# Grouped mixture-of-experts on sorted tokens: five slots of 128 tokens in place of sixteen experts on all 256, and the split of the down weights moved to GpSimd

## The chip, the cores and the metric

One core of a Trainium2 chip runs the whole program in one launch. The metric is device time in microseconds (us), less is better. TensorE does the matmuls, VectorE and ScalarE the elementwise work, GpSimd little, SyncE issues most DMAs. In the profile they are PE (PEld for its weight loads), DVE, ACT, POOL and SP; a "q" behind an engine's name is its instruction queue.

## The reference, cut to what matters

Two layers (projections, retention, windowed and latent attention, layer norm, mixture of experts, layer norm) and one block of another kind (attention, a linear recurrence, an MLP) run over 256 tokens of width 1024, in fp32. The change touches the experts of the two layers:

```python
def grouped_moe(x, router_w, router_bias, w_gate_up, w_down):   # 256 tokens, D = 1024
    scores = sigmoid(t @ router_w)                  # 16 experts in 4 groups of 4
    biased = scores + router_bias
    grp_score = sum(top_k(biased by group, 2))
    sel_group = argmax(grp_score)                   # one group for each token
    top_idx = top_k(biased inside that group, 2)    # two experts of that group
    gates = one_hot(top_idx) * scores / their sum
    h = einsum('td,edf->tef', t, w_gate_up)         # every expert: 1024 -> 2 x 256
    a = silu(h[..., :256]) * h[..., 256:] * gates
    y = einsum('tef,efd->td', a, w_down)            # 256 -> 1024, summed over experts
```

All of a token's weight lies on two experts of one group; for the other fourteen its gate is zero.

## The kernel before, in words

A Fori loop over the two layers holds all engines' programs; the last block follows it. Big matmuls take each fp32 operand as a rounded fp32r part ("high") and the rest ("low") and add three products: high by high, high by low, low by high. So every weight block of 128x2048 is loaded from HBM (by SP, into a half of WE), rounded by ScalarE (`high_up` L654, `high_down` L658), and its rest is taken by VectorE as a `tensor_tensor` subtract with both inputs in SBUF (`low_up` L1539, `low_down` L1543).

For each of the 16 experts all 256 tokens are computed. `expert_up` makes gate and up with the weights stationary and the tokens moving (96 matmuls of 256 columns); ScalarE takes silu (L798); VectorE multiplies with the gate values (L1669) and with the up part (L1673) and splits the result (L1534, L1535). `expert_down` adds 24 matmuls of 512 columns into four banks, y0 to y3, that stay open over all experts. `split_product` and `split_down` call `product`, whose matmul is L990. TensorE's program interleaves experts (`expert_up(m, 0)`, `expert_down(m - 1, 1)`, ...), and three pairs of high and low buffers (gate, up, down) make the other engines wait for TensorE and for one another. Gate values go by DRAM: transposed by TensorE (L1301), written out and broadcast back by two DMAs of the ACT queue (L785, L789).

SP loads an expert's gate and up (2 MB) in one DMA and its down (1 MB) in another, each as soon as the rest of the expert two before is taken (L456, L460). Before the experts come layer norm 1, `transpose_rows("x1T", ...)`, the router product (L990 on `small`), and the selection on VectorE (L1638 to L1664). `keep_warm(job, l, n)` issues n fp32 matmuls of 128 columns on an identity (L1031); an fp32 matmul is two instructions in the trace. After the experts `layer_norm` adds y0 to y3 (L1469 to L1483), and the next layer starts with loads into WE, `high_unit` (L691), `low_unit` (L1558 on VectorE, L547 on GpSimd) and `transpose_rows("xT", ...)`.

GpSimd's program: two `low_unit`, small loads, four `low_unit`, rotary products (L569 to L589), for each layer; then a memset of `w_bd` (L594) and 18 small DMAs (L599, L612) for the last block, on whose `final_in` ScalarE and VectorE wait before its first row is normed; then `low` of the last block's projections (L619).

Of the kernel before, what the change touches and what calls it, by code (L numbers as in the profile page):

```python
# [8 lines left out]
P = 128  # L9
SEQ, D, NL = 256, 1024, 2  # L10
T = SEQ // P
KD = D // P
# [5 lines left out]
PER_GRP = N_EXP // N_GRP  # L18
ST_H, CONV, D_FF, LRU_W = 8, 4, 4096, 512
# [40 lines left out]
    ("router", 0), ("gatesT", 1),  # L60
    ("y0", 0), ("y1", 1), ("y2", 2), ("y3", 3),
    ("gate0", 4), ("up0", 5), ("gate1", 6), ("up1", 7),
# [26 lines left out]
REPEATED = {"gate0": N_EXP // 2, "up0": N_EXP // 2, "gate1": N_EXP // 2, "up1": N_EXP // 2,  # L89
            "ff0": N_CHUNK // 2, "ff1": N_CHUNK // 2}  # L90

# [11 lines left out]
def tables():  # L103
# [26 lines left out]
    for e in range(PER_GRP):  # L130
# [9 lines left out]
        "before": (i < j).astype(np.float64),  # L140
        "tie": np.broadcast_to(tie.reshape(1, -1), (P, PER_GRP * PER_GRP)),
# [22 lines left out]
def build(nc, a, out):  # L164
    ctx = ExitStack()
    with ctx:
# [25 lines left out]
        small = sb("small", [P, 1400])  # L192
# [19 lines left out]
        QL = [over("QL0", "WA", UNIT, [P, KD, 256]), over("QL1", "XT", 0, [P, KD, 256]), over("QL2", "AC", AC_LATE + UNIT, [P, KD, 256])]  # L212
        HIDH = [over(f"HIDH{s}", "XT", s * 1024, [P, 2, SEQ]) for s in range(2)]
# [28 lines left out]
        for s in range(2):  # L242
            ar = Arena(WE, s * E_SLOT)
            w_gu.append(ar.take(KD, 2 * D_EXP))
            w_dn.append(ar.take(D_EXP // P, D))
        w_gate, w_up = ([w[:, :, n * D_EXP:(n + 1) * D_EXP] for w in w_gu] for n in range(2))
# [11 lines left out]
        ar = Arena(WB)  # L258
        gates_b = ar.take(N_EXP, SEQ)
        sig = [ar.take(512) for _ in range(2)]  # L260
        gatesT = ar.take(SEQ)
        assert ar.at <= 3 * UNIT
# [41 lines left out]
        gsel, esel, gden, gates = ar.take(8), ar.take(8, 4), ar.take(2), ar.take(2, N_EXP)  # L304
        n1g, n2g = ar.take(KD), ar.take(KD)
# [4 lines left out]
        rss, marks = ar.take(T), ar.take(8 + T + 2 + T)  # L310
# [4 lines left out]
        gates_dram = nc.dram_tensor("gates_scratch", [NL, N_EXP, SEQ], F32, kind="Internal").ap()  # L315
# [40 lines left out]
        norms_in, ln1_in, ln2_in, gates_in, gates_out = (sem(n) for n in ("norms_in", "ln1_in", "ln2_in", "gates_in", "gates_out"))  # L356
        gu_in, dn_in = [sem(f"gu_in{s}") for s in range(2)], [sem(f"dn_in{s}") for s in range(2)]
# [13 lines left out]
        gates_ready, expert_used = sem("gates_ready"), sem("expert_used")  # L371
# [4 lines left out]
        xt_high, xt_low = sem("xt_high"), sem("xt_low")  # L376
# [21 lines left out]
        DVE_LINKS, POOL_LINKS, MOE_LINKS = 32, 2, 2  # L398

        SLOT_UNITS = (N_EXP + 1, N_EXP, N_EXP - 1, 0)  # L400

        def unit(slot, l, e):
            return l * SLOT_UNITS[slot] + e + 1 if SLOT_UNITS[slot] else e + 1
# [7 lines left out]
        def hidden(l, e):  # L411
            return l * N_EXP + e + 2
# [5 lines left out]
        def _(sp):  # L418
            for t in range(T):
                sp.dma_start(X[:, t, :], a["x"][0, t * P:(t + 1) * P, :]).then_inc(x_in[t], 16)  # L420
            with sp.Fori(0, NL) as l:
# [3 lines left out]
                sp.wait_ge(hid_ready, l * N_EXP + 1)  # L425
# [3 lines left out]
                sp.wait_ge(psum_read[3], l * per_layer[3] + 1)  # L429
# [25 lines left out]
                def load_gate_up(e, s):  # L455
                    sp.dma_start(w_gu[s], a["exp_w_gate_up"][bass.ds(l, 1), bass.ds(e, 1)].rearrange(  # L456
                        "o e (p k) n -> p (o e k) n", k=KD)).then_inc(gu_in[s], 16)

                def load_down(e, s):
                    sp.dma_start(w_dn[s], a["exp_w_down"][bass.ds(l, 1), bass.ds(e, 1)].rearrange(  # L460
                        "o e (c p) n -> p (o e c) n", p=P)).then_inc(dn_in[s], 16)

                for s in range(2):
                    load_gate_up(s, s)
                    load_down(s, s)
# [3 lines left out]
                with sp.Fori(1, N_EXP // 2) as m:  # L469
                    for s in range(2):  # L470

                        sp.wait_ge(low_made[1], unit(1, l, 2 * m + (s - 2)))
                        load_gate_up(2 * m + s, s)

                        sp.wait_ge(low_made[2], unit(2, l, 2 * m + (s - 2)))
                        load_down(2 * m + s, s)
            w2 = a["w_in_2"][0].rearrange("(p k) n -> p k n", k=KD)
            for p, col in enumerate(PROJ_PAIRS):
                if p < 2:

                    sp.wait_ge(low_made[1], unit(1, NL - 1, N_EXP - 2 + p))
# [52 lines left out]
        def _(pool):  # L534
# [5 lines left out]
            with pool.Fori(0, NL) as l:  # L540
# [51 lines left out]

            pool.wait_ge(k_roped, NL + 1)
# [45 lines left out]
        def _(act):  # L639
# [20 lines left out]
            def split_xt(prefix, l):  # L660
                for n in range(4):
# [1213 lines left out]
```

## Time and profile before

| | us |
|---|---|
| median of 3 runs (lowest, highest) | 1242.46 (1239.92, 1244.7) |
| profiled execution, its own time | 1242.1 |
| its span in the trace | 1240.4 |
| PE busy in the span | 1187.7 (96%) |
| DVE, ACT, POOL busy | 641.2, 464.5, 157.2 |
| mean granted clock of TensorE, share of full | 0.986 |
| DMA traffic | 193.94 MB |

Read: the first two lines are times of the whole program; the span is what the trace shows of it. Busy TensorE is not TensorE at its peak, since a matmul's row is longer than the step from one matmul to the next.

### The profile page before, as it was taken

How to read it: one execution, taken by the hardware profiler on the slowest of the kernel's cores; microseconds unless marked ns; L12 is line 12 of the kernel's file. 1: busy time of each engine (PE TensorE's matmuls, PEld its weight loads, DVE VectorE, ACT ScalarE, POOL GpSimd, SP SyncE). 2: the span in 40 equal slices, each digit the busy share in tenths (PEclk: the TensorE clock that was granted, in tenths of full speed). 3: DMA queues.
4: the chain of work that ended last, by engine and by line, in shares of the span. 5: the costliest groups of instructions: out<-in, count | busy, mean ns of one | idle time of the engine just before them, and what ended most of it. 6: DMA issues, size and time to landing. Idle time of an engine off the chain costs nothing.

```text
span 1240.4 us, 19509 instructions
## 1 busy us (share of the span) xinstructions
PE 1187.7 (96%) x7992; PEld 1057.1 (85%) x7992; DVE 641.2 (52%) x721; ACT 464.5 (37%) x533; POOL 157.2 (13%) x90
## 2 busy tenths in 40 slices
PE   8997999999999999996999999999999989999998
PEld 8985579999999989965498999999989865899997
DVE  2226566565555554056566655555564843655653
ACT  3423323333333333432333333333343864443431
POOL 2433000000000003616000000000046420000000
PEclk9997999999999999997999999999999999999999
DMA  9702634554444338107254554445414035355431
GB/s 314 195 2 87 252 103 171 203 203 193 162 161 194 135 105 237 67 1 235 113 192 183 203 198 164 158 190 203 169 35 170 1 136 203 136 203 195 170 141 68
DMA packets 78562, 193.94 MB, mean 156 GB/s; under 512 B 17648, under 2 KB 48544, under 8 KB 74032
## 3 DMA queue, kind: packets, MB, share of 16 engines
q1 hardware_dynamic: 76368, 184.23, 40.8%
q10 hardware_dynamic: 640, 6.27, 1.3%
q0 software_dynamic: 1504, 2.73, 0.9%
q8 instruction: 36, 0.59, 0.2%
q14 instruction: 14, 0.11, 0.0%
HBM read 192.14 MB, written 1.08 MB: 156 GB/s over the span
## 4 chain that ended last, share of the span: by engine, by line
PE 80%; DVE 7%; issue 6%; ACT 3%; DMA 2%; POOL 1%; DVEq 0%; POOLq 0%; ACTq 0%
PE bank L990 73%; PE bank L1031 2%; DMA WB<-gates_scratch 1%; DVE LNB L1791 1%; PE bank L1083 1%; DVE WA L1517 1%; DMA gates_scratch<-WB 1%; DVE AC L1749 1%; PE bank L1065 1%; POOL QL L547 1%; PE bank L1044 0%; ACT WH L654 0%; PE bank L1190 0%; PE bank L1059 0%; PE bank L1069 0%
## 5 line engine op out<-in xcount | busy, mean ns | idle before, releaser
L990 PE MATMUL bank<-XTH,WH 128*128 128x256 f32 x1280 | 362.8, 283 | 1.3 <-DVE XTL L1734 0.8
L990 PE MATMUL bank<-XTH,WL 128*128 128x256 f32 x1280 | 362.2, 283 | 0.0
L990 PE MATMUL bank<-XTL,WH 128*128 128x256 f32 x1280 | 362.2, 283 | 0.0
L990 PEld LDWEIGHTS bank<-XTH,WH 128*128 128x128 f32 x1280 | 245.5, 192 | 3.5 <-issue 1.0
L990 PEld LDWEIGHTS bank<-XTL,WH 128*128 128x128 f32 x1280 | 245.5, 192 | 1.6
L990 PEld LDWEIGHTS bank<-XTH,WL 128*128 128x128 f32 x1280 | 245.5, 192 | 0.0
L1539 DVE TENSOR_TENSOR WL<-WE,WH 128x2048 fp32r<-128x2048 f32 x80 | 183.1, 2291 | 38.3 <-ACT WH L654 36.3
L654 ACT CAST WH<-WE 128x2048 fp32r<-128x2048 f32 x80 | 151.9, 1903 | 105.7 <-PE bank L990 95.3
L1543 DVE TENSOR_TENSOR WL<-WE,WH 128x2048 fp32r<-128x2048 f32 x48 | 109.9, 2290 | 85.4 <-ACT WH L658 85.4
L990 PE MATMUL bank<-WH,HIDH 128*128 128x512 f32 x384 | 150.3, 391 | 3.1 <-DVE HIDL L1535 1.8
L658 ACT CAST WH<-WE 128x2048 fp32r<-128x2048 f32 x48 | 91.5, 1906 | 158.1 <-PE bank L990 149.2
L990 PE MATMUL bank<-WL,HIDH 128*128 128x512 f32 x384 | 149.9, 390 | 0.0
L990 PE MATMUL bank<-WH,HIDL 128*128 128x512 f32 x384 | 149.4, 389 | 0.0
L547 POOL TENSOR_TENSOR QL<-WE,QH 128x2048 fp32r<-128x2048 f32 (+2 forms) x12 | 48.5, 4060 | 414.4 <-ACT QH L691 414.4
L619 POOL TENSOR_TENSOR PL<-WE,PH 128x2048 fp32r<-128x2048 f32 x10 | 46.7, 4676 | 364.5 <-ACT PH L833 364.5
L990 PEld LDWEIGHTS bank<-WH,HIDH 128*128 128x128 f32 x384 | 72.3, 188 | 17.6 <-issue 2.2
L990 PEld LDWEIGHTS bank<-WH,HIDL 128*128 128x128 f32 x384 | 72.1, 188 | 15.3
L990 PEld LDWEIGHTS bank<-WL,HIDH 128*128 128x128 f32 x384 | 72.3, 188 | 13.3
L1031 PE MATMUL bank<-tab 128*128 128x128 f32 x536 | 67.5, 286 | 7.2 <-DMA tab<-in_tables 5.4
L1031 PEld LDWEIGHTS bank<-tab 128*128 128x128 f32 x536 | 66.0, 203 | 9.2 <-issue 9.1
L990 PE MATMUL bank<-WB,XT 128*128 128x512 f32 x160 | 70.0, 595 | 3.6 <-ACT XT L757 1.7
L990 PE MATMUL bank<-XTH,QH 128*128 128x256 f32 x224 | 64.0, 286 | 1.3 <-POOL QL L547 0.8
(288 smaller groups left out, 1626.6 us busy)
## 6 DMA issues: line engine op xcount, KB each, us to landing
WE<-in_exp_w_gate_up SPq DMA_DIRECT2D x32, 2048.0 KB, 9.0
WE<-in_exp_w_down SPq DMA_DIRECT2D x32, 1024.0 KB, 4.9
WE<-in_w_up SPq DMA_DIRECT2D x16, 1024.0 KB, 5.2
WE<-in_w_down SPq DMA_DIRECT2D x16, 1024.0 KB, 5.6
WE<-in_w_in SPq DMA_DIRECT2D x7, 2048.0 KB, 9.4
WE<-in_w_in SPq DMA_DIRECT2D x8, 1024.0 KB, 8.7
WB<-in_w_out SPq DMA_DIRECT2D x2, 2560.0 KB, 10.5
WB<-gates_scratch ACTq DMA_DIRECT2D x2, 2048.0 KB, 8.6
```

What stands on the lines that cost most here:

```text
L547: nc.gpsimd.tensor_tensor(QL[u % 3][:, :, 0:w], raw_unit(u), QH[u % 3][:, :, 0:w].bitcast(F32), ALU.subtract).then_inc(unit_low[u % 3], 1)
L619: nc.gpsimd.tensor_tensor(PL[u % 3][:, :, :], raw, PH[u % 3][:, :, :].bitcast(F32), ALU.subtract).then_inc(proj_low[u % 3], 1)
L654: nc.scalar.copy(WH_up[slot], raw).then_inc(high_made[slot], 1)
L658: nc.scalar.copy(WH_dn[slot], w_dn[s]).then_inc(high_made[slot], 1)
L990: ins = nc.tensor.matmul(dst, lhsT, rhs, start=first and n == 0, stop=last and n == len(pairs) - 1)
L1031: nc.tensor.matmul(bank(job)[:, 0:P], ident, ident, start=True, stop=True)
L1065: nc.tensor.matmul(dst, v0, pT[:, 0:2 * P], start=True, stop=False)
L1083: ins = nc.tensor.matmul(tile_of(job, h % 2), qT[:, P:2 * P], kT, start=True, stop=True)
L1517: v.tensor_scalar(p1[:, h, :], p1[:, h, :], rin[name][:, 1, h:h + 1], None, ALU.mult).then_inc(normed[name], 1)
L1539: v.tensor_tensor(WL_up[slot], raw, WH_up[slot].bitcast(F32), ALU.subtract).then_inc(low_made[slot], 1)
L1543: v.tensor_tensor(WL_dn[slot], w_dn[s], WH_dn[slot].bitcast(F32), ALU.subtract).then_inc(low_made[slot], 1)
L1749: ins = v.scalar_tensor_tensor(conv_u[:, c, :], src, tap, conv_u[:, c, :], ALU.mult, ALU.add)
```

## The change

Tokens are sorted by group. From the group choice, TensorE counts each token's rank in its group (`rank`: 5 small fp32 products), and VectorE builds `SEL`, a 0/1 matrix of 256 tokens by five slots of 128 places: one slot for each group, and a fifth for what is over 128 in one group (one group at most can have more). TensorE gathers the tokens into the slots by matmuls with `SEL` (`g0` to `g7`, `go0`, `go1`), transposes `SEL` and gathers the gate values (`sgate`). Each slot runs the four experts of its group: 20 units, of which the fifth slot's load their weights by a group number read into a register. A unit has tokens stationary and weights moving: 24 matmuls of 512 columns for gate and up together, two transposes of the hidden rows, 12 matmuls of 512 columns for down. The slots' sums are split and put back in token order by 40 matmuls with `SELT` (`scatter`).

Weights come in blocks of 1 MB: A and B (the two halves of gate and up) and D (down), in the order A(n), B(n), D(n-2), in a ring of six raw blocks and a ring of four high and low pairs. ScalarE rounds all three. VectorE takes the rests of A and B, GpSimd those of D. ScalarE rounds a block when TensorE is done with the block four before it. The Fori loops over layers and experts are written out (`for l in range(NL)`); the trips through DRAM are gone.

```diff
+N_PAIR, N_RAW = 4, 6
+        at["A", n], at["B", n], at["D", n] = 3 * n, 3 * n + 1, 3 * (n + 2) + 2
...
 @@ sync
+                def load_block(kind, n, group):
+                    b = BLOCK_AT[kind, n]
+                    if b - N_RAW in BLOCKS:
+                        sp.wait_ge(*rested(b - N_RAW, l))
...
+                    sp.dma_start(dst, src).then_inc(blk_in[b % N_RAW], 16)
+                first = [("A", 0), ("B", 0), ("A", 1), ("B", 1), ("D", 0), ("D", 1), ("A", 2), ("B", 2)]
...
 @@ gpsimd, at the end of a layer and ahead of w_bd and the 18 DMAs
+                for n in [*range(N_UNIT - 2), N_UNIT - 1, N_UNIT - 2]:
+                    b = BLOCK_AT["D", n]
+                    pool.wait_ge(*rounded(b, l))
+                    nc.gpsimd.tensor_tensor(BL[b % N_PAIR][:, :], raw[b % N_RAW], BH[b % N_PAIR][:, :].bitcast(F32), ALU.subtract
+                                            ).then_inc(blk_low[b % N_PAIR], 1)
...
 @@ scalar
+                def high_block(kind, n):
+                    b = BLOCK_AT[kind, n]
+                    act.wait_ge(*on_raw(b, l))
+                    if turn_of(b, N_PAIR) > 1:
+                        act.wait_ge(*done_with(max(c for c in BLOCKS if c < b and c % N_PAIR == b % N_PAIR), l))
+                    nc.scalar.copy(BH[b % N_PAIR][:, :], raw[b % N_RAW]).then_inc(blk_high[b % N_PAIR], 1)
...
+                for n in range(N_UNIT):
+                    if n + 1 < N_UNIT:
+                        if n > 0:
+                            high_block("A", n + 1)
+                        high_block("B", n + 1)
+                    else:
+                        high_block("D", n)
+                    gate_of(n)
+                    if n >= 1:
+                        high_block("D", n - 1)
+                        hidden_high(n - 1)
+                    if n >= 5 and (n - 5) % PER_GRP == 0:
+                        slot_high((n - 5) // PER_GRP)
...
 @@ tensor
+                keep_warm("rank", l, 26)
...
+                product(ranks[:, 0:N_GRP], [(before, first_tile)])
+                product(ranks[:, N_GRP:2 * N_GRP], [(ones, first_tile), (before, second_tile)])
+                product(ranks[:, 2 * N_GRP:3 * N_GRP], [(ones, first_tile), (ones, second_tile)]).then_inc(*made("rank"))
+                keep_warm("g0", l, 10)
+                pe.wait_ge(rows_low, (l + 1) * T)
+                pe.wait_ge(sel_made, (l + 1) * T)
...
+                for n in range(N_UNIT):
+                    unit_up(n)
+                    if n >= 1:
+                        hidden_T(n - 1)
+                    if n >= 2:
+                        unit_down(n - 2)
...
+                for n in range(2):
+                    scatter(n, range(N_GRP))
+                hidden_T(N_UNIT - 1)
+                unit_down(N_UNIT - 2)
+                for n in range(2, 4):
+                    scatter(n, range(N_GRP))
+                unit_down(N_UNIT - 1)
+                for n in range(4):
+                    if n < 2:
+                        pe.wait_ge(*read(f"sy{n}", l, N_GRP))
+                    scatter(n, range(N_GRP, N_SLOT))
...
 @@ vector
+                def low_block(kind, n):
+                    b = BLOCK_AT[kind, n]
+                    dve.wait_ge(*rounded(b, l))
+                    v.tensor_tensor(BL[b % N_PAIR][:, :], raw[b % N_RAW], BH[b % N_PAIR][:, :].bitcast(F32), ALU.subtract
+                                    ).then_inc(blk_low[b % N_PAIR], 1)
...
+                for n in range(N_UNIT):
+                    if n + 1 < N_UNIT:
+                        if n > 0:
+                            low_block("A", n + 1)
+                        low_block("B", n + 1)
+                    gated(n)
+                    if n >= 1:
+                        hidden_low(n - 1)
+                    if n >= 5 and (n - 5) % PER_GRP == 0:
+                        slot_low((n - 5) // PER_GRP)
```

`gated`, `hidden_low` and `slot_low` have one input in PSUM and one in SBUF. The constant table grows by 128 columns.

## Rows read from the trace of the kernel before

**Rows 1.** The page: span, busy time of the engines.

```profile
span 1240.4 us, 19509 instructions
PE 1187.7 (96%) x7992; PEld 1057.1 (85%) x7992; DVE 641.2 (52%) x721; ACT 464.5 (37%) x533; POOL 157.2 (13%) x90
```

**Rows 2.** Chain that ended last: start us, us, what.

```profile
206.67 246.19 PE bank L990 x1716
```

**Rows 3.** Windows: busy us of each engine, PEclk, DMA share, GB/s.

```profile
207.00:440.00 233.00, 233.00 (x1643) 219.60 (x1642) 130.85 (x99) 84.56 (x56) 0.00 (x0) 1.00 0.43 167
124.00:140.00 16.00, 14.80 (x85) 11.06 (x85) 7.59 (x11) 7.29 (x30) 0.00 (x0) 0.95 1.02 426
104.00:108.00 4.00, 2.72 (x26) 2.35 (x25) 3.68 (x9) 0.00 (x0) 3.70 (x2) 1.00 0.01 4
```

**Rows 4.** PE around the end of layer 1's experts: start us, us, engine line.

```profile
453.14 0.39 PE L990 MATMUL bank<-WH,HIDL 128*128 128x512 f32 x1
...
455.18 0.39 PE L990 MATMUL bank<-WH,HIDL 128*128 128x512 f32 x1
...
460.21 3.29 PE L1031 MATMUL bank<-tab 128*128 128x128 f32 x28
463.34 1.06 PE L1044 MATMUL bank<-tab,X 128*128 128x128 f32 x8
464.24 4.63 PE L1031 MATMUL bank<-tab 128*128 128x128 f32 x40
```

**Rows 5.** Groups by form: busy us, mean ns of one, idle before.

```profile
L1539 DVE TENSOR_TENSOR WL<-WE,WH 128x2048 fp32r<-128x2048 f32 x80 | 183.1, 2291 | 38.3 <-ACT WH L654 36.3
L654 ACT CAST WH<-WE 128x2048 fp32r<-128x2048 f32 x80 | 151.9, 1903 | 105.7 <-PE bank L990 95.3 <-DMA gates_scratch<-WB 10.4
L547 POOL TENSOR_TENSOR QL<-WE,QH 128x2048 fp32r<-128x2048 f32 x8 | 36.7, 4609 | 33.0 <-ACT QH L691 33.0
L1578 DVE SCALAR_TENSOR_TENSOR WB<-bank,small,WB 128x256 f32<-128x256 f32 x10 | 4.1, 478 | 35.7 <-ACT WB L724 35.7
L775 ACT COPY XT<-bank 128x512 f32<-128x512 f32 x4 | 2.1, 588 | 10.2 <-PE bank L1044 10.2
```

**Rows 6.** PE and DVE from the router on, layer 0.

```profile
178.12 3.72 PE L990 MATMUL bank<-small,XT 128*128 128x16 f32 x32
181.70 0.36 PE L990 MATMUL bank<-XTH,WH 128*128 128x256 f32 x1
...
184.60 0.17 DVE L1655 TENSOR_SCALAR small<-small 128x8 f32<-128x8 f32 x1
...
186.53 0.20 DVE L1659 TENSOR_TENSOR small<-small 128x32 f32<-128x32 f32 x1
```

**Rows 7.** POOL, then DVE, at the start of layer 1.

```profile
469.22 3.52 POOL L547 TENSOR_TENSOR QL<-WE,QH 128x1536 fp32r<-128x1536 f32 x1 [353.83 <-ACT QH L691]
...
468.68 2.47 DVE L1565 TENSOR_TENSOR XTL<-bank,XTH 128x512 fp32r<-128x512 f32 x4
471.07 3.81 DVE L1558 TENSOR_TENSOR QL<-WE,QH 128x2048 fp32r<-128x2048 f32 x1
```

**Rows 8.** POOL, then DVE, in the last block.

```profile
980.01 9.46 POOL L619 TENSOR_TENSOR PL<-WE,PH 128x2048 fp32r<-128x2048 f32 x2 [9.90 <-ACT PH L833]
...
978.95 11.07 DVE L1791 TENSOR_TENSOR_SCAN LNB<-AC 128x256 f32<-128x256 f32 x4
```

**Rows 9.** DVE at the end of layer norm 2, layer 0.

```profile
457.10 0.68 DVE L1469 SCALAR_TENSOR_TENSOR X<-X,bank 128x512 f32<-128x512 f32 x1
...
461.43 1.28 DVE L1483 SCALAR_TENSOR_TENSOR X<-X,small,LNB 128x1024 f32<-128x1024 f32 x1
```

**Rows 10.** POOL: the memset and the last four of 18 small DMAs.

```profile
565.37 0.98 POOL L594 MEMSET w_bd<- 128x1024 f32 x1
...
575.29 3.02 POOL L612 DMA_DIRECT2D small<-in_conv_w  x4
```

**Rows 11.** DMA issues: KB each, median us to landing.

```profile
small<-in_conv_w POOLq DMA_DIRECT2D x4, 2.0 KB, 6.2
```

More of the change, by code:

```diff
@@ L816, in _ @@
-                expert_step(0, 0, first=True)
-                with act.Fori(1, N_EXP // 2) as m:
-                    expert_step(m - 1, 1)
-                    expert_step(m, 0)
-                expert_step(N_EXP // 2 - 1, 1, last=True)
+                high_block("A", 1)
+                for k in range(KD):
+                    act.wait_ge(*full(f"g{k}", l))
+                    dst = XS_ALL[:, :].rearrange("p (g q) -> p g q", g=N_GRP)[:, :, k * P:(k + 1) * P]
+                    nc.scalar.copy(dst, bank(f"g{k}")[:, :].rearrange("p (g q) -> p g q", g=N_GRP)).then_inc(gathered, 1)
@@ new lines, in _, with gate_of @@
+                for half in range(2):
+                    act.wait_ge(*full(f"go{half}", l))
+                    nc.scalar.copy(XS[N_GRP][:, half * 512:(half + 1) * 512], bank(f"go{half}")[:, :]).then_inc(gathered, 1)
+                for n, w in ((0, 512), (1, 512), (2, 256)):
+                    act.wait_ge(*full(f"selT{n}", l))
+                    nc.scalar.copy(SELT[:, n * 512:n * 512 + w], bank(f"selT{n}")[:, 0:w]).then_inc(*took(f"selT{n}"))
+                def gate_of(n):
+                    job = f"gu{n % 2}"
+                    act.wait_ge(*full(job, l, n // 2))
+                    nc.scalar.activation(hsig[n % 2], bank(job)[:, 0:D_EXP], ACT.Silu).then_inc(silu_done, 1)
@@ L1096, in _ @@
             pe.wait_ge(ident_in, 16)
-            with pe.Fori(0, NL) as l:
+            for l in range(NL):
                 transpose_rows("xT", X, l, x_ready, l * T, "lat0", (8, 14))
@@ new lines, in _, with gather @@
+                pe.wait_ge(sel_made, (l + 1) * T)
+                def gather(dst, k, cols):
+                    return product(dst, [pair for t in range(T) for pair in (
+                        (X1H[:, t, k:D:KD], SEL[:, t, cols]), (X1L[:, t, k:D:KD], SEL[:, t, cols]))])
+                for k in range(KD):
+                    pe.wait_ge(*free(f"g{k}", l))
+                    gather(bank(f"g{k}")[:, :], k, slice(0, N_GRP * P)).then_inc(*made(f"g{k}"))
+                for half in range(2):
+                    pe.wait_ge(*free(f"go{half}", l))
+                    for k in range(4 * half, 4 * half + 4):
+                        ins = gather(tile_of(f"go{half}", k % 4, P), k, slice(N_GRP * P, N_SLOT * P))
+                    ins.then_inc(*made(f"go{half}"))
```

445 lines of the change are left out of this document (263 added, 182 removed), and 4 rows, old and new, of the table LAYER_JOBS.

## The prediction, made before the changed kernel was run

> **What bounds the kernel now.** I read the page first: a span of 1240.4 us, PE busy in 96% of it [rows 1]. The chain of waits then has one unbroken piece of TensorE's L990 of 246.19 us in the experts of layer 1 [rows 2], with a second of the same length for layer 2. The windows confirm it: from 207 to 440 us PE is busy in all of the 233.00 us, DVE in 131, ACT in 85, POOL in nothing, DMA at a share of 0.43 [rows 3]. So the experts are bound by TensorE's columns alone. The stage to beat: the router product ends at 181.70 [rows 6], the last down product at 455.4 [rows 4], and layer norm has its last row ready at 461.43 + 1.28 = 462.7 [rows 9].
>
> The step from one 512-column product to the next is (455.18 - 453.14) / 9 = 0.227 us; a 128-column one steps by (463.34 - 460.21) / 28 = 0.112 [rows 4].
>
> **The new routing, per layer.** I follow it from 181.7, on layer 1's clock. TensorE: `keep_warm("rank", 26)` is 52 instructions x 0.112 = 5.8, to 187.5; the group choice it waits for is there at 184.8 [rows 6], so the warming itself is on the path. Rank: five fp32 products, ten instructions, 1.1 -> 188.7. VectorE had nothing left after 186.7 [rows 6]; four small ops of 0.2 and a hop -> 189.6. `SEL` is new: 2 x 640 columns; at 2291 / 2048 = 1.12 ns a column [rows 5] some 0.8 each -> 191.4 with a hop. Were one input's broadcast dear, twice that, +1.6. Gather: 32 x 0.227 = 7.3; fifth slot 32 x 0.112 = 3.6; ten transposes 1.1; gate gather, 20 instructions at 3.72 / 32 = 0.116 [rows 6], 2.3 -> 205.7. ScalarE copies a gathered bank in 0.59 [rows 5] and VectorE subtracts in about 0.7, both under the 0.91 that TensorE needs for a bank: hidden. The DRAM trip and its transposes go; they were on the chain, but TensorE had products to run meanwhile, so I credit nothing. Routing: 24.0 us in which the old kernel was already multiplying.
>
> **The units.** TensorE needs 36 x 0.227 + 2 x 0.112 = 8.4 us a unit. ScalarE: three roundings of 1.90 [rows 5], silu, hidden and slot copies, about 6.9. VectorE: two rests of 2.29 and some 1.2 of small ops, 5.8. GpSimd: one rest of 4.61 [rows 5]. DMA: 3.15 MB. Each alone is under 8.4.
>
> But VectorE and GpSimd are not independent. At the start of layer 2 a 128x2048 rest on VectorE took 3.81 instead of 2.29. A GpSimd rest was running from 469.22 to 472.74; 472.74 + 2.29 is 475.0, and the VectorE op ended at 474.9 [rows 7]: it stood until GpSimd was through. In the last block four scans of 256 columns took 11.07 beside two GpSimd rests of 9.46 in all [rows 8]. Just before the blocked op, four subtracts with one input in PSUM kept their 0.62 each beside the same GpSimd op [rows 7], and L1578, likewise with a PSUM input, averages 0.48 [rows 5]. So what excludes is two SBUF inputs. The Trainium skill ("SBUF — State Buffer", "Who interferes with whom") says the same: such a VectorE instruction contends with a GpSimd instruction that reads SBUF, and the loser fully blocks; the rule speaks against moving D to GpSimd, and the trace agrees.
>
> The rests of a unit therefore queue on one thing: 2 x 2.29 + 4.61 = 9.2 us, more than TensorE's 8.4. All on VectorE they would have been 6.9, and VectorE about 8.1. `gated`, `hidden_low` and `slot_low` have a PSUM input and fit beside GpSimd. Is the shared path always asked for? A block may be rounded when the block four before it is used, so when TensorE starts D(n), A, B and D of the next unit can be rounded: yes, nearly. Carrying four units, with the turn going to whoever waits, I get 37.4 us, 9.35 a unit: 9.2 and 0.17 idle. Ends of the range for this term: 9.2 (no idle) and 10.1 (below).
>
> Sum: the first demand is B(1)'s rest, at 205.7 + 2.7 (A(0) multiplied) + 1.9 + 0.2 = 210.5. From there 37 x 2.29 + 20 x 4.61 = 176.9, plus 1.8 at the start until A(2) and D(0) are rounded, plus 18 x 0.17 = 3.1: D(18)'s rest, last on GpSimd, ends at 392.3. Behind it `unit_down(18)` 2.7, 16 scatter products 3.6, `unit_down(19)` 2.7 -> 401.4. The last slot's copy and rest cannot be hidden: 0.6 + 0.7 + hops, 1.5; then the last eight products -> y1 at 403.35, y3 at 404.3. Layer norm got its parts well apart before; now y0 to y3 come within 1.4 us, so it is serial: 4.1 for the first rows and 462.7 - 457.1 = 5.6 for the second [rows 9] -> 413.0, against 462.7. Gain 49.7 a layer, of which 3 us less than the matmuls won is lost in this tail.
>
> **What is moved past.** GpSimd's `w_bd` memset and 18 small DMAs now stand behind D(18) of layer 2 instead of in its middle. From 392.3: 0.98 + 0.3 + 11.7 for the issues (to 575.29 + 3.02 = 578.3 from 566.6) [rows 10] + 6.2 to land [rows 11] = 411.5, where ScalarE asks for them at about 411.0: +0.5 once. If issue slows beside VectorE, up to 6. SP's next-layer loads into WE come earlier than before; the first product of the layer waits for rows, not for them, so nothing. The table's 64 KB at 426 GB/s [rows 3] is +0.15. The layer loop's branches go; TensorE is in a warming stretch until 468.9 there [rows 4], so at most -0.5, taken as 0.
>
> **Total:** -2 x 49.7 + 0.7 = -98.7. The profiled execution took 1242.1 (span 1240.4), the median is 1242.46, so nothing needs scaling: 1143.
>
> **Rivals.**
> B, no exclusion between these ops: TensorE's 8.4 holds. GpSimd's chain still fits (B used at 5.5, silu 0.4, rounding 1.9, rest 4.6, needed at 14.1). 205.7 + 168 + 1.3 (first D) + 9.1 (scatter) + 2.0 (D(18)) + 1.5 = 387.6, 16.7 earlier than 404.3 a layer: 1110. For it: POOL spans are rough. Against: the blocked op [rows 7] and the scans [rows 8].
> C, the path is idle between its users, since ScalarE rounds in order and GpSimd's turn delays the A or B that TensorE needs next: 0.75 more a unit, 10.1, x 38: 1172. For it: each late rest delays TensorE, and thereby the next rounding.
> D, DMA: 3.15 MB in 9.35 us is 336 GB/s. The rows give 426 with a full queue and 167 / 0.43 = 388 at full share [rows 3]. A quarter below 388, 291 GB/s, makes 10.8 a unit and 1201.
> The Trainium skill ("DMA: Bandwidth & Descriptors", "Where 436 GB/s comes from") gives about 358 GB/s of HBM for a core: 8.8 a unit, which would leave my sum and lift B by 15; the 426 measured speaks against it.
> E, slower: TensorE's clock. It fell to half in this kernel just after 104 to 108 us, where PE was busy 2.72 of 4 us [rows 3]. With gaps in every unit, the clock at 1.2 GHz makes a unit 16.8 us, 7.45 over my 9.35; 98.7 / 7.45: from 13 of the 40 units on, the change loses. With half of them 1292. Against it: a unit's gap is 0.9 us of 9.35, dense products otherwise.
>
> **How the numbers follow.** Forecast 0.58 (1133 to 1155), B 0.12, C 0.19 (1156 to 1185), D 0.07, E 0.04. The range 1108 to 1178 takes in the forecast, B and most of C, about 0.83. Measurements of this kernel tell about 0.5% from no change, 6 us. All cases but E are faster: 0.95; E slower: 0.04; within 0.5%: 0.01, where C and D meet.
>
> **What would show it.** Right: 40 POOL rests of 4.6 to 5 us; of VectorE's block rests a third or more at 4 to 7 us instead of 2.29, and about none of ACT's roundings longer than 1.9; units 9.2 to 9.5 apart; PE waiting on POOL's or DVE's rests about 0.9 us a unit; unit_up(0) 24 us after the router. Wrong: VectorE rests all at 2.29 and units 8.4 apart (B); units over 9.8 with the path idle (C); ACT's roundings waiting for DMA (D); PEclk under 0.9 among the units (E).

## The result, and the profile after

The median of the kernel after is 1185.78 us (1181.23 to 1187.39, 4 runs), beside 1242.66 of the kernel before (1239.92 to 1244.7, 4 runs): a ratio of 0.9538, 95% interval 0.9505 to 0.9571. It is faster, by 56.9 us and not by the 98.7 of the forecast, and 7.8 us above the range. The profiled execution took 1181.23; the other three were 3.6 to 6.2 us slower, so traces below are compared with traces, and medians with medians.

The page of the kernel after, beside [rows 1] and [rows 5]:

```profile
span 1179.4 us, 14703 instructions
...
PE 1089.1 (92%) x6100; PEld 916.1 (78%) x6100; DVE 677.4 (57%) x723; ACT 538.4 (46%) x644; POOL 368.2 (31%) x130
...
L674 POOL TENSOR_TENSOR BL<-WE,BH 128x2048 fp32r<-128x2048 f32 x40 | 210.4, 5262 | 377.6 <-ACT BH L777 377.6
L1797 DVE TENSOR_TENSOR BL<-WE,BH 128x2048 fp32r<-128x2048 f32 x80 | 276.7, 3495 | 40.0 <-ACT BH L777 39.8
L777 ACT CAST BH<-WE 128x2048 fp32r<-128x2048 f32 x120 | 228.4, 1907 | 79.5 <-PE bank L1082 58.6
```

GpSimd has the 40 down rests, 5.26 us each (4.61 for one of this shape before), and VectorE's mean rest went from 2.29 to 3.50. Both grew, as the prediction said the exclusion would show, though GpSimd's go past its 4.6 to 5 us (the longest takes 6.75). ScalarE's rounding kept its 1.91. TensorE is busy 92% of the span.

Where the chain that ended last had one piece of 246 us in layer 1's experts [rows 2], it now changes hands. Five of its pieces there (start us, us, what), and the window of layer 1's experts with the columns of [rows 3]:

```profile
209.59 17.73 PE bank L1082 x68
...
231.63 11.37 DVE BL L1797 x2
...
295.11 12.47 DVE BL L1797 x2
...
350.89 12.45 DVE BL L1797 x2
...
401.14 8.97 POOL BL L674 x2
```
```profile
207.00:434.00 227.00, 203.62 (x871) 165.88 (x872) 166.31 (x113) 131.75 (x118) 104.26 (x20) 0.91 0.73 263
```

TensorE is without work for 23 of these 227 us, and its clock stands at 0.91. Three times the chain goes through a pair of VectorE's rests that takes 11 to 12.5 us, and at the end through two rests of GpSimd.

I cut each layer at four points: the end of the router product, the first product of unit 0, the end of D(17)'s rest on GpSimd, and the rows that layer norm 2 hands on. The prediction has the same four points: 24.0 us of routing, 177.4 to D(17)'s rest (205.7 to 383.1), 29.9 to the rows.

| stretch, us | forecast | after, layer 1 | after, layer 2 |
|---|---|---|---|
| routing: 180.66 to 213.51 | 24.0 | 32.9 | 31.2 |
| units: 213.51 to 393.48 | 177.4 | 180.0 | 178.3 |
| tail: 393.48 to 433.73 | 29.9 | 40.2 | 40.3 |
| sum | 231.3 | 253.1 | 249.9 |

(Times in the first column are layer 1's.) The excess is 21.8 and 18.6, together 40; the profiled run is 38 over the forecast. Nearly all of it lies in the routing and in the tail. The units are where they were put.

**The units.** Timelines of GpSimd, VectorE and TensorE in the middle of layer 1 (start us, us, ..., idle before and its releaser):

```profile
283.65 6.31 POOL L674 TENSOR_TENSOR BL<-WE,BH 128x2048 fp32r<-128x2048 f32 x1 [2.53 <-ACT BH L777]
292.07 6.72 POOL L674 TENSOR_TENSOR BL<-WE,BH 128x2048 fp32r<-128x2048 f32 x1 [2.12 <-ACT BH L777]
300.81 4.60 POOL L674 TENSOR_TENSOR BL<-WE,BH 128x2048 fp32r<-128x2048 f32 x1 [2.01 <-ACT BH L777]
...
295.11 12.46 DVE L1797 TENSOR_TENSOR BL<-WE,BH 128x2048 fp32r<-128x2048 f32 x2
...
307.62 0.56 PE L1082 MATMUL bank<-BH,XS_ALL 128*128 128x512 f32 x1 [2.99 <-DVE BL L1797]
```

and TensorE's windows around that wait (busy us, PEclk, DMA share, GB/s):

```profile
304.00:308.00 4.00, 1.01 (x5) 0.99 0.39 158
308.00:311.00 3.00, 3.00 (x9) 0.50 0.81 246
311.00:314.00 3.00, 3.00 (x15) 0.95 1.00 408
```

The pattern repeats every six or seven units. TensorE goes at 8.42 us a unit. One GpSimd rest and two of VectorE, queueing on each other, take 8.84 (GpSimd's rests end at 254.57, 263.43, 272.27, ...; the 9.2 of the forecast is a little too much). So each GpSimd rest starts against a longer queue and grows by 0.42: 4.63 us at 249.94, then 5.07, 5.47, 5.90, 6.31, 6.72. When the slack is used up the turns change: VectorE's two rests stand behind one GpSimd operation each and take 12.46 instead of 4.58, and TensorE waits 2.99 for one of them. Behind that wait its clock is at half for 3.4 us. The whole costs one unit 13.7 to 14.6 us from one hidden transpose to the next, and the slack is there anew. The second unit, 14.7, is long by the start as well (see "GpSimd busy as long, but only writing").

Over 17 units, without the first and the last, the mean is 9.50 in layer 1 and 9.44 in layer 2; the forecast had 9.35. Layer 1's 9.50 is 9.01 in which a rest runs on one of the two engines, and 0.49 in which none does; the forecast's was 9.2 and 0.17. TensorE's own count of the same 18.3 us over 8.42 a unit is 10.2 us of waits for rests, and most of the other 8 is the clock at half behind the three waits of 3 us.

**The routing.** The weight loads of the gather in the group view, by form (count, busy us, mean ns):

```profile
L1082 PEld LDWEIGHTS bank<-SEL,X1L 128*128 128x128 f32 x32 | 10.7, 335 | 0.0
```

and windows of layer 1 for PE alone (busy us, PEclk, DMA share, GB/s):

```profile
201.00:203.00 2.00, 2.00 (x10) 1.00 0.00 0
205.00:207.00 2.00, 2.00 (x10) 0.63 0.00 0
207.00:209.00 2.00, 2.00 (x11) 0.50 0.04 8
213.00:215.00 2.00, 2.00 (x8) 0.50 0.93 389
217.00:219.00 2.00, 2.00 (x6) 0.50 0.00 0
219.00:221.00 2.00, 2.00 (x9) 0.96 0.00 0
```

A stationary tile of X1H or X1L is every eighth of 1024 columns, and its load takes 0.335 us; contiguous ones take 0.19 to 0.20. So the 32 products of the fifth slot step by 0.242 us instead of 0.112 (199.70 to 207.43), and the 512-column ones by 0.245 instead of 0.227. The gather took 15.8 us, not 10.9. From 205.5, still among the fifth slot's products, to 219 TensorE's clock is at half, 1.2 GHz, while its busy share is full all the time: the transposes and the gate gather took 6.1 instead of 3.4, and unit 0 ran its first half at that clock.

**The tail.** Timelines of SP, ACT, POOL and PE at the end of layer 1's experts:

```profile
393.65 0.37 SPq L537 DMA_DIRECT2D WE<-in_exp_w_down  x1
...
399.16 1.90 ACT L777 CAST BH<-WE 128x2048 fp32r<-128x2048 f32 x1 [10.68 <-DMA WE<-in_exp_w_down]
...
401.24 1.89 ACT L777 CAST BH<-WE 128x2048 fp32r<-128x2048 f32 x1
...
401.14 8.96 POOL L674 TENSOR_TENSOR BL<-WE,BH 128x2048 fp32r<-128x2048 f32 x2 [7.66 <-ACT BH L777]
...
410.15 0.79 PE L1082 MATMUL bank<-BH,HTH 128*128 128x512 f32 x1 [7.74 <-POOL BL L674]
```

ScalarE rounds D(19) before D(18), and GpSimd rests them in that order. D(19)'s raw slot is D(17)'s; SP may load it when D(17)'s rest is done (393.48), and it lands at 399.1. ScalarE idled 10.68 us for it with D(18) lying ready behind, so D(18)'s rest ended 16.6 us behind D(17)'s instead of 9.2, and TensorE waited 7.74 for it. The clock was at half again from 403.5 to 413.7.

### The profile page after: what moved, and what is told of

It is laid out like the page before. It is cut to its first block, busy times and chain, and to the rows that moved or that the text cites. A ratio compares the mean times of both kernels' runs of the same rounds, so it can differ in the third digit from the quotient of the medians.

```text
span 1179.4 us, 14703 instructions
## 1 busy us (share of the span) xinstructions
PE 1089.1 (92%) x6100; PEld 916.1 (78%) x6100; DVE 677.4 (57%) x723; ACT 538.4 (46%) x644; POOL 368.2 (31%) x130
## 4 chain that ended last, share of the span: by engine, by line
PE 75%; DVE 14%; ACT 5%; POOL 3%; DMA 1%; issue 1%; ACTq 0%; DVEq 0%; SPq 0%
PE bank L1082 63%; DVE BL L1797 6%; PE bank L1123 5%; POOL BL L674 2%; ACT BH L777 2%; DVE WA L1689 1%; DVE LNB L2000 1%; PE bank L1175 1%; PE bank L1136 1%; DMA WE<-in_exp_w_down 1%; DVE AC L1958 1%; PE bank L1157 1%; PE bank L1433 0%; PE bank L1282 0%; DVE small L1644 0%
## 5 line engine op out<-in xcount | busy, mean ns | idle before, releaser
L674 POOL TENSOR_TENSOR BL<-WE,BH 128x2048 fp32r<-128x2048 f32 x40 | 210.4, 5262 | 377.6 <-ACT BH L777 377.6
L1797 DVE TENSOR_TENSOR BL<-WE,BH 128x2048 fp32r<-128x2048 f32 x80 | 276.7, 3495 | 40.0 <-ACT BH L777 39.8
L777 ACT CAST BH<-WE 128x2048 fp32r<-128x2048 f32 x120 | 228.4, 1907 | 79.5 <-PE bank L1082 58.6
L1082 PE MATMUL bank<-BH,XS_ALL 128*128 128x512 f32 x512 | 172.1, 408 | 12.1 <-DVE BL L1797 12.1
L1082 PEld LDWEIGHTS bank<-BH,XS_ALL 128*128 128x128 f32 x512 | 101.6, 198 | 35.5 <-DVE BL L1797 13.8
L1082 PE MATMUL bank<-BL,XS_ALL 128*128 128x512 f32 x256 | 103.8, 405 | 0.0
L1082 PE MATMUL bank<-BH,HTH 128*128 128x512 f32 x160 | 67.8, 424 | 18.3 <-POOL BL L674 17.9
L1082 PE MATMUL bank<-XTH,WH 128*128 128x256 f32 x256 | 72.6, 284 | 0.8 <-DVE XTL L1943 0.8
L1082 PE MATMUL bank<-XTL,WH 128*128 128x256 f32 x256 | 72.4, 283 | 0.0
L1082 PE MATMUL bank<-XTH,WL 128*128 128x256 f32 x256 | 72.4, 283 | 0.0
L1082 PEld LDWEIGHTS bank<-WB,XT 128*128 128x128 f32 x160 | 30.0, 190 | 40.3 <-issue 40.3
```

The costliest lines, as they stand in the source:

```text
L674: nc.gpsimd.tensor_tensor(BL[b % N_PAIR][:, :], raw[b % N_RAW], BH[b % N_PAIR][:, :].bitcast(F32), ALU.subtract).then_inc(blk_low[b % N_PA ...
L777: nc.scalar.copy(BH[b % N_PAIR][:, :], raw[b % N_RAW]).then_inc(blk_high[b % N_PAIR], 1)
L1082: ins = nc.tensor.matmul(dst, lhsT, rhs, start=first and n == 0, stop=last and n == len(pairs) - 1)
L1797: v.tensor_tensor(BL[b % N_PAIR][:, :], raw[b % N_RAW], BH[b % N_PAIR][:, :].bitcast(F32), ALU.subtract).then_inc(blk_low[b % N_PAIR], 1)
```

## The experiments

Three edits undo one of these each: the exclusion (rests on VectorE), the stride, the order. Then they are put together. "The kernel after" is the base of every diff.

### Rests of the down blocks on VectorE

GpSimd's loop over the down blocks is gone, and VectorE's over the units has them:

```diff
-                for n in [*range(N_UNIT - 2), N_UNIT - 1, N_UNIT - 2]:
-                    b = BLOCK_AT["D", n]
-                    pool.wait_ge(*rounded(b, l))
-                    nc.gpsimd.tensor_tensor(BL[b % N_PAIR][:, :], raw[b % N_RAW], BH[b % N_PAIR][:, :].bitcast(F32), ALU.subtract
-                                            ).then_inc(blk_low[b % N_PAIR], 1)
...
                         low_block("B", n + 1)
+                    else:
+                        low_block("D", n)
                     gated(n)
                     if n >= 1:
+                        low_block("D", n - 1)
                         hidden_low(n - 1)
```

> The kernel after, but the rests of the down blocks are taken by VectorE in the order in which ScalarE rounds them, and GpSimd does nothing in the experts. Theory (a VectorE operation and a GpSimd operation that both have two SBUF inputs exclude each other): the rests of the A and B blocks fall from a mean of 3.5 us to 2.29, D rests take 2.29, a unit takes TensorE's 8.43 instead of 9.2 to 9.5, and of the 180.0 us from unit_up(0) to the rest of D(17) some 15 go, with 2 to 4 more at the tail, where D(19) and D(18) cost 2.3 each instead of 4.5: 1150, or 1145 to 1157. Rival 1 (the units are held by ScalarE's order of rounding or by the loads, which GpSimd's part does not touch): the rests shorten but the units stay 9.2 to 9.5 apart, and the time stays within 1180 to 1190. Rival 2 (VectorE becomes the bound with three rests of 2.29 and its small operations, 8.1 us a unit by my sum and more if an operation waits for its PSUM input): units of 8.9 to 9.2 with VectorE busy over 0.95, 1165 to 1180.

1132.56 us (1132.01 to 1134.73); ratio to before 0.9127, 0.9108 to 0.9147. That beats the kernel after by 53 us. The group of the rests from 200 to 430 us:

```profile
L1792 DVE TENSOR_TENSOR BL<-WE,BH 128x2048 fp32r<-128x2048 f32 x58 | 132.2, 2290 | 23.2 <-ACT BH L772 22.1
```

and the window of 260 to 300 us (busy us of PE, PEld, DVE, ACT, POOL, then PEclk, DMA share, GB/s):

```profile
260.00:300.00 40.00, 40.00 (x182) 32.97 (x181) 37.66 (x28) 31.26 (x28) 0.00 (x0) 1.00 1.00 374
```

All rests take 2.29, all units 8.41, and VectorE is busy 0.94 of the time without delaying anybody. That fits the exclusion, but GpSimd also has nothing to do here; the next run takes its reading and its being busy apart. Rival 1 falls, since the loads moved 374 GB/s here and held nobody; rival 2 falls on the spacing. The gain was larger than I wrote: 21.7 us of layer 1's 180.0 (158.3), not 15, because the first units gain too, and 3.2 of its tail.

The Trainium skill ("SBUF — State Buffer", "Who interferes with whom") says that a VectorE instruction with two SBUF inputs contends with a GpSimd instruction that reads SBUF and not with one that only writes it; this run and the kernel after, 2.29 against 3.50, agree with the first half.

### GpSimd busy as long, but only writing

Left out: the rests of the down blocks but for 16 columns. (`cleared` counts the clears, so that each waits for the one before it.)

```diff
-                    nc.gpsimd.tensor_tensor(BL[b % N_PAIR][:, :], raw[b % N_RAW], BH[b % N_PAIR][:, :].bitcast(F32), ALU.subtract
+                    for _ in range(5):
+                        pool.wait_ge(cleared, n_cleared)
+                        nc.gpsimd.memset(w_bd[:, :, :, :], 0.0).then_inc(cleared, 1)
+                        n_cleared += 1
+                    nc.gpsimd.tensor_tensor(BL[b % N_PAIR][:, 0:16], raw[b % N_RAW][:, 0:16], BH[b % N_PAIR][:, 0:16].bitcast(F32),
```

> The kernel after, but in place of each rest of a down block GpSimd clears the block-diagonal tile five times and subtracts 16 of the 2048 columns: it is busy about as long (estimate 5 to 5.5 us a block, five times the 0.98 of its memset and a small operation) but hardly reads SBUF. Left out: the rests of the down blocks but for their first 16 columns. Theory (what excludes is two SBUF inputs on both engines): VectorE's rests of A and B take 2.29 in the mean, not 3.5, and the units go at TensorE's 8.43; 1140 to 1158. Rival 1 (a GpSimd that gives the down block 5 us late holds the units, through the order in which blocks come free): the rests of VectorE are 2.29, but the units stay at 9.2 to 9.5; 1175 to 1190. Rival 2 (GpSimd's writes exclude VectorE as well): rests of 3.5 us or more, units of 9.2 or more, 1180 or more.

1160.37 us (1159.25 to 1161.5, 2 runs); 25 us less than the kernel after, just outside my bounds. Groups of 205 to 390 us:

```profile
L678 POOL MEMSET w_bd<- 128x1024 f32 x94 | 89.9, 956 | 180.9 <-ACT BH L784 176.6
L1804 DVE TENSOR_TENSOR BL<-WE,BH 128x2048 fp32r<-128x2048 f32 x38 | 86.9, 2292 | 47.0 <-ACT BH L784 47.0
```

and, from TensorE's timeline, the end of its wait in the second unit:

```profile
234.72 0.80 PE L1089 MATMUL bank<-BH,HTH 128*128 128x512 f32 x1 [3.04 <-POOL BL L680]
```

with GpSimd's 16 columns of D(0) and of D(1), from its own timeline:

```profile
233.13 1.53 POOL L680 TENSOR_TENSOR BL<-WE,BH 128x16 fp32r<-128x16 f32 x1
...
239.56 0.22 POOL L680 TENSOR_TENSOR BL<-WE,BH 128x16 fp32r<-128x16 f32 x1
```

GpSimd was busy 86.9 us of the 150 from 220 to 370, and VectorE's 38 rests still took 2.29 each. So it is GpSimd's reading that excludes, as the second half of that rule has it, and a busy GpSimd does not hold the units: all but the second go at 8.41 between the first and the last. That one takes 13.15 (8.41 with the rests on VectorE): D(0) is rounded only at 228.0, and GpSimd hands it over at 234.7. Of these 6.7 us 5.0 are the five clears, and 1.5 the small subtract, which takes 0.22 otherwise: it reads, and it stood until VectorE's two rests ended at 234.6. So the 4.7 us a layer at the start are in the main the latency of a slow GpSimd and its consequences, with 1.3 of contention in them. I had missed it.

The run is 29 us above the one with the rests on VectorE (profiled executions): in layer 1 7.7 in the units, 5.7 in the tail and 1.6 in the routing. So of what moving the rests to VectorE gained, ending the exclusion alone gives 14.0 of 21.7 us in layer 1's units and 25 of 53 in the medians. The rest comes with a GpSimd that takes longer for a block (here 5.2 us) than VectorE's 2.29 and hands it over late; how it splits further was not measured.

### Half of the down rests on GpSimd

```diff
-                for n in [*range(N_UNIT - 2), N_UNIT - 1, N_UNIT - 2]:
+                for n in range(0, N_UNIT, 2):
...
+                    else:
+                        low_block("D", n)
                     gated(n)
                     if n >= 1:
+                        if (n - 1) % 2 == 1:
+                            low_block("D", n - 1)
                         hidden_low(n - 1)
```

> The kernel after, but only the down blocks of even units have their rests on GpSimd; those of odd units are taken by VectorE in ScalarE's order. Theory (a queue of all rests on one path): two units ask the path for 5 x 2.29 + 4.6 = 16.05 us, less than the 16.86 that TensorE needs, so the units go at 8.43 and the time is that of all rests on VectorE with 0 to 5 more for the tail and for the waits of single rests: 1132 to 1142. Rival 1 (the sum is not the bound, but every turn of GpSimd costs the path an idle stretch or delays the block needed next): half of the loss between the kernel after and the one with all rests on VectorE stays, 1150 to 1165. Rival 2 (VectorE with five rests in two units and its small operations is now behind where GpSimd blocks it): 1165 or more.

1138.36 us (1137.14 to 1140.1), inside the bounds of the theory of one queue. The groups of 205 to 390 us:

```profile
L1797 DVE TENSOR_TENSOR BL<-WE,BH 128x2048 fp32r<-128x2048 f32 x48 | 124.0, 2611 | 27.0 <-ACT BH L777 27.0
...
L674 POOL TENSOR_TENSOR BL<-WE,BH 128x2048 fp32r<-128x2048 f32 x10 | 47.0, 4703 | 226.5 <-ACT BH L777 226.5
```

Single VectorE rests are still blocked (mean 2.61), but all units except the second (9.73) take 8.41. Half the load costs 6 us against the 53 of the whole: with a sum of rests of 16.05 in TensorE's 16.86, the units behind the second lose nothing. What is left lies in the second unit, 1.3 us a layer, and in the tail, where D(18)'s rest is GpSimd's 4.54 instead of 2.29.

### Gathered rows written by feature

```diff
+        def by_k(w, t):
+            return w[:, t, :].rearrange("p (k m) -> p m k", k=KD)
-                    nc.scalar.copy(X1H[:, t, :], X[:, t, :])
+                    nc.scalar.copy(by_k(X1H, t), X[:, t, :].rearrange("p (m k) -> p m k", k=KD))
-                        (X1H[:, t, k:D:KD], SEL[:, t, cols]), (X1L[:, t, k:D:KD], SEL[:, t, cols]))])
+                        (X1H[:, t, token(k)], SEL[:, t, cols]), (X1L[:, t, token(k)], SEL[:, t, cols]))])
```

X1L is written in the same way.

> The kernel after, but ScalarE and VectorE write X1H and X1L with the columns of a block of 128 features together, so that each stationary tile of the gather is 128 columns in a row instead of every eighth of 1024. Same results. Theory (the weight load of a strided tile, 0.335 us instead of 0.19, sets the step of the gather): the 512-column gather step falls from 0.245 to 0.227, the fifth slot's from 0.242 to about 0.12, together 0.6 + 3.9 = 4.5 us a layer, 9 in all: 1177, or 1174 to 1180; if the clock then also holds through the rest of the routing, 2 to 3 us more a layer, down to 1170. The layer norm's last copy and rest, now with a strided output, may cost up to 0.5 us a layer. Rival (the step of the fifth slot comes from waits on PSUM banks or from the clock, not from the load): the load falls, the step stays near 0.24, 1182 to 1187.

1162.17 us (1160.52 to 1164.38); ratio 0.9368, 0.9347 to 0.9388: 23.6 us less than the kernel after, and 8 below my lowest. The load of a tile, in the group view:

```profile
L1085 PEld LDWEIGHTS bank<-SEL,X1L 128*128 128x128 f32 x32 | 6.1, 190 | 0.6
```

and windows from the fifth slot into unit 0 (columns as in the window before):

```profile
200.00:204.00 4.00, 4.00 (x37) 3.95 (x36) 2.08 (x3) 1.33 (x4) 0.00 (x0) 1.00 0.00 0
204.00:207.00 3.00, 3.00 (x30) 3.00 (x29) 2.43 (x2) 1.80 (x4) 0.00 (x0) 1.00 0.02 5
207.00:218.00 11.00, 11.00 (x51) 9.07 (x51) 6.24 (x10) 7.30 (x5) 0.00 (x0) 1.00 0.51 175
```

The load fell to 0.190, the gather to 11.06 us (192.86 to 203.92; forecast 10.9), the fifth slot's step to 0.111. And the clock stayed at 2.4 GHz through the transposes (3.1 us instead of 6.1) and unit 0 (11.0 to its hidden transposes instead of 13.6). That second part, 5.6 us a layer, is what I had put at 2 to 3. In both layers of all five kernels with strided tiles the clock fell at the end of the gather; in both layers of the three without, and with 26 warming products, it did not. Whether the slow loads or something else in that stretch brings it down wasn't tried apart.

The Trainium skill ("SBUF — State Buffer", "Door 1: The DMA port swizzle") has a note that consecutive reads of SBUF are at full bandwidth if at least two hit the same 16 bytes, and that fp32 can be strided by 4 for free. The stride here is 8, and 0.335 against 0.190 us agrees; no run has another stride. The prediction should have weighed it and didn't.

### D(18) before D(19)

```diff
-                for n in [*range(N_UNIT - 2), N_UNIT - 1, N_UNIT - 2]:
+                for n in range(N_UNIT):
...
-                    else:
-                        high_block("D", n)
                     gate_of(n)
...
+                high_block("D", N_UNIT - 1)
                 hidden_high(N_UNIT - 1)
```

VectorE's signal that frees the raw blocks for the next layer's loads now waits for both last rests.

> The kernel after, but at the end of the experts ScalarE rounds D(18) before D(19), and GpSimd takes their rests in that order. Theory (D(18), which TensorE needs first, stands behind D(19), whose raw slot comes free only with D(17)'s rest and whose load takes 5.5 us from there): D(18)'s rest ends at about 393.5 + 4.5 to 5, some 11 us earlier than the 410.1 of now; D(19)'s load lands at 399 as before and its rest ends at about 401.1 + 4.5 = 405.6, when TensorE has done unit_down(18) and the scatter (398.5 + 2.7 + 3.6 = 404.8): the last product comes some 6 to 8 us earlier a layer, 1167 to 1174. Rival (the load of D(19) does not hang on D(17)'s rest, but lands late with all loads of the queue, and D(18) too): D(18) is rounded no earlier, gain under 2 us a layer, 1181 to 1187.

1157.33 us (1156.7 to 1162.81); ratio 0.9336, 0.9307 to 0.9365: 28.5 us less in the median, 24.1 in the profiled executions. Timelines of ScalarE and GpSimd at the tail of layer 1:

```profile
392.90 1.91 ACT L777 CAST BH<-WE 128x2048 fp32r<-128x2048 f32 x1
...
398.55 1.90 ACT L777 CAST BH<-WE 128x2048 fp32r<-128x2048 f32 x1 [3.48 <-DMA WE<-in_exp_w_down]
...
394.88 4.60 POOL L674 TENSOR_TENSOR BL<-WE,BH 128x2048 fp32r<-128x2048 f32 x1 [2.90 <-ACT BH L777]
```

The window from 404 to 408 us, first of this kernel:

```profile
404.00:408.00 4.00, 4.00 (x19) 3.34 (x18) 0.06 (x1) 0.43 (x1) 1.15 (x1) 1.00 0.20 52
```

then of the kernel after, where TensorE had nothing:

```profile
404.00:408.00 4.00, 0.00 (x0) 0.00 (x0) 0.00 (x0) 0.97 (x1) 4.00 (x2) 0.50 0.01 4
```

D(19)'s load still hangs on D(17)'s rest (issued at 392.15, rounded from 398.55), but D(18) no longer stands behind it: the tail took 29.5 us in place of 40.2, and the forecast was 29.9. I expected 6 to 8 of these 10.7 us. I had left out the clock, which now holds to 416, with TensorE busy all but 0.14 us up to 408; how much of the difference it makes was not measured apart.

### Rows by feature and the order, with GpSimd as it was

The diffs of the two sections above, together.

> The kernel after with X1H and X1L written by features and D(18) before D(19), but the rests of the down blocks still on GpSimd: the kernel as the prediction costed it. Theory (the term of the units was right, and the routing and the order of the tail are the whole miss): the prediction's 1143, or by subtraction of the two single edits from the profiled 1181.2, 1181.2 - 20.7 - 24.1 = 1136; 1133 to 1145, with the units at 9.2 to 9.5. Rival (the units' waits grow by what the routing and the tail give back, since VectorE and GpSimd then meet at other points): 1148 to 1160.

1136.31 us (1132.61 to 1142.31); ratio 0.9164, 0.9131 to 0.9197. This is nearly the kernel that the prediction costed (there D(18) stood last, with both blocks ready), and it lands 6.7 us from the prediction's 1143. Layer 1 took 23.5 us of routing (forecast 24.0), 174.2 to D(17)'s rest (177.4), 29.5 of tail (29.9). The rests:

```profile
L1799 DVE TENSOR_TENSOR BL<-WE,BH 128x2048 fp32r<-128x2048 f32 x80 | 272.5, 3443 | 36.0 <-ACT BH L780 35.8
...
L677 POOL TENSOR_TENSOR BL<-WE,BH 128x2048 fp32r<-128x2048 f32 x40 | 207.7, 5195 | 344.7 <-ACT BH L780 344.7
```

They are as long as in the kernel after, and units still come in groups of 8.42 with one of 12 to 15: a mean of 9.29 over the 17, in both layers.

### All three

The two diffs above and the rests on VectorE, whose last two stand in the new order:

```diff
                     gated(n)
                     if n >= 1:
+                        low_block("D", n - 1)
                         hidden_low(n - 1)
...
+                low_block("D", N_UNIT - 1)
                 hidden_low(N_UNIT - 1)
```

> The kernel after with the three edits at once: rests of the down blocks on VectorE, X1H and X1L written by features, D(18) rounded and rested before D(19). Theory (three independent losses): the profiled execution of the kernel after took 1181.2; the rests on VectorE took 48.6 off in the profiled executions, the rows by feature some 7.5 a layer in the routing, and the order 5 to 6 a layer (D(18)'s rest now stands at 384.7 behind D(19)'s load, and TensorE has nothing from about 382): 1181.2 - 48.6 - 15 - 11 = 1107, or 1102 to 1113. Rival (the gains overlap: what the clock or TensorE loses in one place is only moved): 1115 to 1132.

1104.52 us (1104.02 to 1104.96); ratio to before 0.8895, 0.8875 to 0.8914, and 81 us under the kernel after. From its page:

```profile
span 1102.9 us, 14705 instructions
...
L1794 DVE TENSOR_TENSOR BL<-WE,BH 128x2048 fp32r<-128x2048 f32 x120 | 273.2, 2288 | 28.3 <-ACT BH L775 26.1
```

It is the best of the kernels run here. Routing took 25.1 and 23.5 us, units 8.41. The three single edits took 48.6, 20.7 and 24.1 off the profiled execution, 93.4 in all, and together 76.5: the routing's part adds up, while the rests on VectorE and the order share the tail, as the expectation had it.

### The same with 4 warming products instead of 26

```diff
-                keep_warm("rank", l, 26)
+                keep_warm("rank", l, 4)
```

> The one with all three edits, but with 4 warming products instead of 26 ahead of the rank product. Theory of the prediction (the warming is on the path only for its last 1 us, since the group choice is there 4.8 us after the router product ends; TensorE would be idle for some 4 us instead of busy): if the clock holds through such a gap, 1 to 2 us less than with 26. Rival (the clock falls behind the gap): the gather or what follows runs at half speed for some microseconds, 3 to 8 us a layer, 6 to 16 more than with 26, and PEclk shows 0.5 behind 190.

1105.32 us (1102.72 and 1107.92, 2 runs): the same as with 26. Windows of layer 1 (columns as before):

```profile
183.00:187.00 4.00, 3.66 (x17) 3.69 (x18) 2.99 (x13) 0.00 (x0) 0.00 (x0) 0.50 0.00 0
187.00:191.00 4.00, 4.00 (x18) 3.81 (x18) 1.78 (x7) 0.00 (x0) 0.00 (x0) 0.51 0.02 4
205.00:209.00 4.00, 4.00 (x13) 3.15 (x12) 0.52 (x4) 0.00 (x0) 0.00 (x0) 0.62 0.74 244
```

The clock does fall behind the gap, up to 190.5 and again from 204, as the rival said; layer 2 has the same two falls. But the first mostly meets warming products, and the gather starts 9.5 us behind the router in both layers, against 11.0 and 9.4 with 26. What is gained in one place is lost in the other; two runs 5 us apart can't tell more.

## Why the prediction was wrong

Layer 1 of the forecast and of the kernels, us (rests on V: the down rests on VectorE):

| stretch | forecast | after | rests on V | by feature | order | feature + order | all three |
|---|---|---|---|---|---|---|---|
| routing | 24.0 | 32.9 | 31.2 | 25.5 | 32.9 | 23.5 | 25.1 |
| units | 177.4 | 180.0 | 158.3 | 176.5 | 178.4 | 174.2 | 156.1 |
| tail | 29.9 | 40.2 | 37.1 | 40.8 | 29.5 | 29.5 | 32.2 |

(Where VectorE takes the down rests, D(17)'s ends earlier against TensorE's work, so units look shorter there and the tail longer.)

The direction and the mechanism of the units were right; the size was off by 43 us in the median, in two terms of the sum (the gather, and the time of D(18)'s rest) and in the clock behind them. That the term of the units came out right is in part luck.

- **"Gather: 32 x 0.227 = 7.3; fifth slot 32 x 0.112 = 3.6"** failed. The steps came from rows with contiguous stationary tiles [rows 4]; the new tiles are strided, their load (0.335) is longer than a 128-column product, and it set the step. Measured 15.8 instead of 10.9, 4.9 us a layer. Written by feature: 11.06.
- **"ten transposes 1.1; gate gather 2.3"** failed by the clock: 6.1 instead of 3.4, and 2.6 in unit 0. Rival E looked for the clock among the units, from gaps. It did fall there, at each wait of 3 us, but the mean stayed at 0.95 (214 to 393), above E's 0.9. The larger fall was in the routing, where TensorE had no gap.
- **The start of the routing**, router to the first gather product, was 9.7 by forecast, 11.0 in layer 1 (the clock was partly at half among the warming products) and 9.4 in layer 2. Right. (VectorE's selection runs to 187.6 in the trace before, not to 186.7; the rank product at 188.7 is later than both.)
- **"The rests of a unit therefore queue on one thing"** was right in its cause (rests on VectorE, GpSimd only writing, half on GpSimd). In its size, 9.35 forecast for 9.50 and 9.44, errors cancel: the rests took 9.01 and not 9.2, the idle stretches 0.49 and not 0.17. The second unit alone lost 6.2 us at the start of the queue, where I had 1.8; without it the mean of layer 1 is 9.17. And the picture was too even. I had every unit a little late; in truth TensorE runs at 8.42 on slack and then loses 5 to 6 us at once, 3 of them by a wait and most of the others by its clock.
- **"D(18)'s rest, last on GpSimd, ends at 392.3"** failed. I laid the two last down blocks behind each other with both ready. I did not ask when D(19)'s load could begin: its slot comes free with D(17)'s rest, and the load then takes 5.5 us. That is 7.4 us a layer, and 3 more behind it, of which 1.8 lie in `unit_down(18)`, 4.5 us instead of 2.7 on a clock that had fallen in the gap. In the other order, 29.5 for a forecast of 29.9, with D(18)'s rest 7.5 us behind D(17)'s and not 9.2.
- **Layer norm, serial behind y0 to y3**: the last product with SELT ends at 424.23, rows at 433.73. 9.5 us against the forecast's 8.7 (404.3 to 413.0).
- **The last block's small loads, +0.5**: GpSimd's last issue ends at 841.8 and lands 2.5 us later (6.2 in the forecast); ScalarE's first row of the last block is at 850.8. No delay.
- **Rival B** (no exclusion, 1110) is out by the traces. **Rival C** came nearest in time (1172), mostly by luck: the path was idle for 0.49 us a unit, more than the forecast's 0.17, but not by C's 0.75 more, and the units were not over 9.8. **D** is out: the loads moved 374 to 396 GB/s at full share, and held no unit when VectorE took all rests. (The 358 GB/s of the Trainium skill, "DMA: Bandwidth & Descriptors", "Where 436 GB/s comes from", are given as what a core gets from HBM; this core alone got more, so they are no bound here.)
- **The range** took its width from the bounds of the units' term alone. The routing and the tail, 54 of the 231 us of a layer and mostly new operations, had no bounds of their own but 1.6 for SEL. Both ran over.

## What to carry to other kernels

Take the price of a matmul from a row with the same access pattern of its stationary operand, not only of the same size: a strided tile costs more to load, and a short product can't hide it. Where an engine takes blocks out of order at the end of a stage, ask for each block when its buffer comes free and its load lands; one late block first in line delays the ready ones. Put GpSimd beside two-input VectorE work only up to the point where their sum stays under the engine that bounds the stage: half the down rests cost 6 us here, all of them 53, about half of it by exclusion and the rest by blocks that come late. Where a mean comes out as forecast, look at its parts: here a smaller sum, a longer idle time and a fallen clock gave nearly the same number.

## What the runs showed of the hardware that was not expected

- A weight load of 128x128 fp32r with a stride of 8 elements takes 0.332 to 0.335 us, a contiguous one 0.188 to 0.198.
- TensorE's clock went to half (PEclk 0.50 from 207 to 219, in the kernel after) at the end of a stretch in which its busy share was full: 32 products of 128 columns at steps of 0.242 us. With steps of 0.111 in the same place it stayed at 1.00. A full busy share in the profile is no assurance of the clock.
- It also went to half at single waits of TensorE of 3.0 us among dense products: at 243.1, 307.9 and 362.5 us of layer 1 (the last time within the wait), for 3.4, 3.4 and 6.8 us.
- VectorE and GpSimd do not share the loss evenly: GpSimd's operation grows by 0.42 us a unit over six units, and then a pair of VectorE operations takes 12.46 us at once.
